# GpSimd rounds the gate weights, the compressed scores move into the GLA levels, and a Tanh goes ahead of the logarithms

## The chip, the cores and the metric

The kernel runs on one core of a Trainium2 chip. The metric is the device time of the whole program in microseconds, the median of several runs. Engines run their own instruction streams and meet at semaphores: TensorE (PE), VectorE (DVE), ScalarE (ACT), GpSimd (POOL), and SyncE (SP), which here issues the loads of weights.

## The reference, cut to what matters

The program has two blocks. The change touches only the first one, which runs two layers (`DEPTH = 2`) over 256 tokens of width 1024. One layer is:

```python
def hybrid_layer(x, ...):
    proj = rms_norm(x, norm_mix) @ w_in            # q, k, v, gates of all four mixers
    y_nsa = nsa_mixer(...)        # compressed + selected + window attention, 8 heads
    y_sb  = stick_breaking_mixer(sb_q, sb_k, sb_v)
    y_gla = gla_mixer(...)        # gated linear attention, 4 heads
    y_fox = forgetting_mixer(...)
    branch = einsum('bsnc,ncd->bsnd', stack([y_nsa, y_sb, y_gla, y_fox], axis=2), w_branch)
    gates  = sigmoid(gate_logits + b_gate)         # 4 x 1024 columns of proj
    x = x + sum(gates * branch) @ w_out
    return x + square(relu(rms_norm(x, norm_ff) @ w_ff1)) @ w_ff2

# nsa_mixer, compressed part: 15 compressed keys
s_cmp = einsum('bsghd,bcgd->bghsc', q, kc) * scale
p_cmp = masked_softmax(s_cmp, cmp_end[None, :] <= tok[:, None])
o_cmp = einsum('bghsc,bcgd->bsghd', p_cmp, vc)

# stick_breaking_mixer
sp = where(valid, softplus(z), 0)                  # needs a logarithm
later = cumsum(sp, reverse=True) - sp
a = where(valid, exp(log_sigmoid(z) - later), 0)
```

The second block (a modulated transformer with grouped and latent attention) is not touched by the change.

## The kernel before, in words

**Split products.** A product in float32 is made of three fast matmuls: each weight half tile (256 columns by 8 pieces of 128 rows, 128x2048 in SBUF) is split into a rounded high part and the rest. `Split.make_high` (L233 to L241) rounds on ScalarE into one of two buffers, `ring_high`; `Split.make_low` (L243 to L249) subtracts on VectorE, in place in the ring. Part i may be rounded when TensorE is done with part i-2, since there are two buffers. The parts are numbered: 26 for the projections, then 16 for the eight gate tiles (`GATE_CUT` is 26), then 4 for `w_out` (`OUT_CUT` is 42).

**The order in a layer.** It is written out by hand, engine by engine. TensorE makes the projections. Among those of the stick-breaking and forgetting mixers (names `sq0` to `fv1`) it puts nine *levels* of the gated linear attention (`level(n)`, L724 on). For each level VectorE runs `prepare(n)` (a difference, then, after an Abs and an Exp by ScalarE, two products), `make_low` of the next part, and `merge(n-1)`; ScalarE runs `level_exp`, takes a projection out of PSUM and runs `make_high`. Then come `ff` (two 8-column products per piece), the GLA output `go0`, `go1`, and the sum `fc` for the forgetting mixer.

**The steps.** 16 steps follow (`PAIRS`), m = 0 to 15. Step m has a pair of heads of one kind, in the order slc, win, fox, sb, four times over. In a step TensorE makes two gate projections (`filler`, g0 to g31, 24 matmuls of 256 columns each), the scores of this pair, the transposes (or, for sb, the sums, L842) of the pair before, and the output of the pair before. ScalarE takes each gate projection out of PSUM with a Tanh, makes the exponentials, and on odd fillers rounds a gate part for two steps later. VectorE makes maxima, normalisation and `make_low`. In an sb step ScalarE needs Abs and Exp, then two Ln, and the Ln lie in another function table than Exp and Tanh.

**The compressed scores.** TensorE makes them before the levels, into the two score banks (`cmp0`, `cmp1`). VectorE takes them (L1390) only after the GLA normalisation; s0, s1 of step 0 use the same two banks. TensorE transposes the weights `p_cmp` in step 1 (`turn_compressed`, L793), and ScalarE copies them from there. PSUM banks are used in a fixed rotation (`Banks`): a claim waits until the use two before is freed. g1 uses the bank of `fc`, g8 that of g7.

Of the kernel before, what the change touches and what calls it, by code (L numbers as in the profile page):

```python
# [14 lines left out]
P = 128  # L15
D, S, DEPTH = 1024, 256, 2
KD = D // P
# [189 lines left out]
class Split:  # L207
# [34 lines left out]

    def make_low(self, nc, dve, *which):  # L243
# [51 lines left out]
def first_layer(nc, l, T, dram, out, sem, chip):  # L295
# [91 lines left out]
    for i in range(4 * KD):  # L387
# [5 lines left out]
        if i in ada_steps:  # L393
# [21 lines left out]
               [f"rope{i}" for i in range(3)] + LV + ["p0", "p1"] + [f"pc{g}{i}" for g in range(2) for i in range(2)]  # L415
               + [f"p{j}" for j in soft_jobs[2:]])
# [122 lines left out]
    with nc.Block() as block:  # L539
# [27 lines left out]
        def _(pe):  # L567
# [199 lines left out]

            PT.taken(pe, "lv8_0", "lv8_1")
# [23 lines left out]

            def turn_compressed():  # L793

                for g in range(2):
                    pe.wait_ge(cmp_ready, g + 1)
                    for i in range(2):
                        ps = PT.claim(pe, f"pc{g}{i}")
                        for c in range(2):
                            for t in range(TT):  # L800
                                at = (c * TT + t) * P
                                last = turn(ps[0:N_CMP, at:at + P], p_cmp[:, g, 2 * i + c, t, :])
                        last.then_inc(PT.full, 1)
# [97 lines left out]
            for m in range(PAIRS + 1):  # L901
# [13 lines left out]
                if m == 1:  # L915
                    turn_compressed()
# [62 lines left out]
        def _(act):  # L979
# [115 lines left out]
            for i, (name, out, kw) in enumerate((  # L1095
# [8 lines left out]
                if 2 <= i + 1 <= len(LEVELS) - 2:  # L1104
                    level_exp(i + 1)
            PROJ.taken(act, "ff")
# [11 lines left out]
            for g in range(2):  # L1118
                act.wait_ge(cmp_in, g + 1)
                f(p_cmp[:, g], p_cmp[:, g], ACT.Exp).then_inc(cmp_exp, 1)  # L1120
# [3 lines left out]
            def filler(i):  # L1124
# [3 lines left out]
                if i % 2 == 1 and i < 4 * KD - 4:  # L1128
                    Y.make_high(nc, act, GATE_CUT + 2 + i // 2)
# [23 lines left out]
            def scores(m):  # L1153
                if jobs[2 * m][0] == "sb":
# [4 lines left out]
                    for e in range(2):  # L1159
                        f(sb_u[:, e], sb_u[:, e], ACT.Ln, bias=one).then_inc(sb_log, 1)  # L1160
                    return
                for e in range(2):
# [5 lines left out]
                      accum_out=total[:, e, 1:2]).then_inc(SC.free(f"s{j}"), 1)  # L1168

# [7 lines left out]
            for m in range(PAIRS + 1):  # L1177
# [11 lines left out]
                if m == 1:  # L1189
                    for g in range(2):  # L1190
                        for i in range(2):
                            ps = PT.arrived(act, f"pc{g}{i}")
                            copy(pcT[g][0:N_CMP, 2 * i:2 * i + 2, :], ps[0:N_CMP, :].rearrange("p (c s) -> p c s", c=2))\
                                .then_inc(PT.free(f"pc{g}{i}"), 1)
# [1340 lines left out]
```

## Time and profile before

| | us |
|---|---|
| median of 3 runs | 2514.04 |
| lowest and highest | 2513.93, 2516.71 |
| the profiled execution's own time | 2516.49 |
| its span, first to last instruction | 2514.7 |
| TensorE busy | 2289.3 (91%) |
| VectorE busy | 1122.4 (45%) |
| ScalarE busy | 1084.2 (43%) |
| GpSimd busy | 16.3 (1%) |
| mean granted TensorE clock | 0.96 of full |

The first layer lies at about 25 to 735 us of the span, the second at about 735 to 1450. Within them the levels lie at 133 to 209 and 845 to 921, the steps at 233 to 444 and 945 to 1159. A busy TensorE is not TensorE at its peak: the same matmuls take about twice as long at half the granted clock.

### The profile page before, as it was taken

The numbers are of one execution on the slowest core, as the hardware profiler recorded it, in microseconds if no ns is written. First come the engines' busy times: TensorE is split into PE (matmuls) and PEld (weight loads), VectorE is DVE, ScalarE is ACT, GpSimd is POOL, SyncE is SP. The second block draws the span as 40 slices with busy tenths as digits, with TensorE's granted clock in tenths as the row PEclk, the third lists the DMA queues.
The fourth block names the chain that finished last, engine by engine and source line by source line (L and its number), as shares of the span: only waits on it lengthen the run. The fifth ranks groups of instructions, "written<-read, shape, count | busy, mean of one in ns | idle before, by whom it ended". The sixth has DMA issues, their size and how long they took to land. (4 is left out here: it accounts for less than half of the span.)

```text
span 2514.7 us, 33045 instructions
## 1 busy us (share of the span) xinstructions
PE 2289.3 (91%) x13767; PEld 1845.2 (73%) x13767; DVE 1122.4 (45%) x1582; ACT 1084.2 (43%) x1720; POOL 16.3 (1%) x23
## 2 busy tenths in 40 slices
PE   5998999989969998999899798788999998997998
PEld 4898777879858996778798653445788886454987
DVE  3464333455424544342544312755334435265565
ACT  4444555156323445552464236742332241353553
POOL 0000000000000000000000000000000000100000
PEclk9998999999979998999899989998999999998999
DMA  7532566444446324656445242002222223212442
GB/s 201 200 135 101 197 224 203 175 180 177 167 109 217 131 81 176 216 201 218 167 168 187 80 182 72 2 1 84 101 101 82 86 78 88 71 64 84 167 174 78
DMA packets 197141, 341.19 MB, mean 136 GB/s; under 512 B 45955, under 2 KB 60734, under 8 KB 196862
## 3 DMA queue, kind: packets, MB, share of 16 engines
q1 hardware_dynamic: 194300, 334.68, 38.3%
q0 software_dynamic: 944, 3.47, 0.4%
q8 instruction: 112, 1.84, 0.3%
q10 hardware_dynamic: 1746, 0.89, 0.1%
q14 instruction: 39, 0.32, 0.0%
HBM read 335.88 MB, written 3.15 MB: 135 GB/s over the span
## 5 line engine op out<-in xcount | busy, mean ns | idle before, releaser
L261 PE MATMUL bank<-hT_high,ring_low 128*128 128x256 f32 (+1 forms) x2032 | 609.9, 300 | 0.0
L261 PEld LDWEIGHTS bank<-hT_high,ring_low 128*128 128x128 f32 x2032 | 394.0, 194 | 12.5 <-issue 0.5
L260 PE MATMUL bank<-hT_low,ring_high 128*128 128x256 f32 (+1 forms) x1008 | 300.1, 298 | 19.9 <-ACT work L983 11.7
L262 PE MATMUL bank<-hT_high,ring_high 128*128 128x256 f32 (+1 forms) x1008 | 291.6, 289 | 0.0
L248 DVE TENSOR_TENSOR ring_low<-ring,ring_high 128x2048 fp32r<-128x2048 f32 (+2 forms) x92 | 203.0, 2207 | 190.9 <-ACT ring_high L241 190.5
L260 PE MATMUL bank<-ring_low,hidden_high 128*128 128x512 f32 x640 | 254.3, 397 | 0.0
L241 ACT ACTIVATE ring_high<-ring 128x2048 fp32r<-128x2048 f32 (+2 forms) x92 | 169.2, 1841 | 154.4 <-DMA ring<-w_out 72.1
L260 PEld LDWEIGHTS bank<-hT_low,ring_high 128*128 128x128 f32 (+1 forms) x1008 | 197.4, 196 | 31.1 <-issue 19.6
L983 ACT ACTIVATE work<-bank 128x512 f32<-128x512 f32 (+8 forms) x264 | 120.4, 482 | 215.7 <-PE bank L262 172.4
L248 DVE TENSOR_TENSOR ring_low<-ring,half_high 128x2048 fp32r<-128x2048 f32 x64 | 146.3, 2292 | 136.6 <-ACT half_high L241 136.6
L262 PEld LDWEIGHTS bank<-hT_high,ring_high 128*128 128x128 f32 (+1 forms) x1008 | 196.6, 195 | 0.4
L241 ACT ACTIVATE half_high<-ring 128x2048 fp32r<-128x2048 f32 x64 | 121.7, 1908 | 154.1 <-PE bank L262 154.1
L260 PE MATMUL bank<-hT_low,half_high 128*128 128x512 f32 (+1 forms) x512 | 176.2, 344 | 11.6 <-DVE hT_low L2395 8.2
L262 PE MATMUL bank<-hT_high,half_high 128*128 128x512 f32 (+1 forms) x512 | 174.4, 341 | 0.0
L262 PE MATMUL bank<-half_high,hidden_high 128*128 128x512 f32 x384 | 151.5, 395 | 0.0
L261 PE MATMUL bank<-half_high,hidden_low 128*128 128x512 f32 x384 | 150.7, 392 | 0.0
L1831 PE MATMUL bank<-work,ring 128*128 128x512 f32 (+3 forms) x384 | 141.5, 524 | 6.8 <-DVE work L2241 3.7
L983 ACT ACTIVATE work<-bank,work 128x256 f32<-128x256 f32 (+1 forms) x200 | 88.1, 460 | 134.3 <-PE bank L262 95.5
L2065 ACT ACTIVATE work<-bank 128x512 f32<-128x512 f32 (+3 forms) x145 | 79.4, 584 | 143.3 <-PE bank L1831 140.7
L260 PEld LDWEIGHTS bank<-ring_low,hidden_high 128*128 128x128 f32 x640 | 120.2, 188 | 26.3
L569 PE MATMUL bank<-work 64*128 64x128 f32 (+8 forms) x1032 | 118.7, 334 | 21.3 <-DVE work L1390 14.9
L1831 PE MATMUL bank<-work 128*64 128x256 f32 (+5 forms) x550 | 111.7, 455 | 14.0 <-DVE work L2282 6.7
(214 smaller groups left out, 4153.1 us busy)
## 6 DMA issues: line engine op xcount, KB each, us to landing
ring<-w_ff SPq DMA_DIRECT2D x32, 2048.0 KB, 8.3
ring<-mlp_w SPq DMA_DIRECT2D x32, 2048.0 KB, 8.2
ring<-w_in SPq DMA_DIRECT2D x30, 2048.0 KB, 7.8
ring<-w_ada SPq DMA_DIRECT2D x24, 2048.0 KB, 7.9
ring<-w_branch SPq DMA_DIRECT2D x6, 2048.0 KB, 10.7
ring<-w_in SPq DMA_DIRECT2D x32, 256.0 KB, 4.2
ring<-w_out SPq DMA_DIRECT2D x4, 2048.0 KB, 7.7
ring<-gqa_w_qkv SPq DMA_DIRECT2D x3, 2048.0 KB, 15.6
```

Of the source, the lines that this page charges most:

```text
L241: nc.scalar.activation(self.high(i), self.part(i, False), ACT.Copy).then_inc(self.high_made, 1)
L248: nc.vector.tensor_tensor(self.part(i, True), self.part(i, False), self.high(i).bitcast(F32), ALU.subtract)\
L260: nc.tensor.matmul(out, a[0], b[1], start=start, stop=False)
L261: nc.tensor.matmul(out, a[1], b[0], start=False, stop=False)
L262: return nc.tensor.matmul(out, a[0], b[0], start=False, stop=stop)
L569: return nc.tensor.matmul(out, lhsT, rhs, start=start, stop=stop)
L983: return nc.scalar.activation(out, in_, func, **kw)
L1831: return nc.tensor.matmul(o, lhsT, rhs, start=start, stop=stop)
L2065: return f(o, src, ACT.Copy, **kw)
```

## The change

Three things are moved. (1) Of the 16 gate parts, ScalarE still rounds the first two; the other 14 are rounded by a copy on GpSimd, in a block of its own. (2) The work on the compressed scores goes into the GLA levels on VectorE and ScalarE; TensorE transposes `p_cmp` right behind `ff`, ahead of the GLA output, and ScalarE's four copies stand ahead of the `log_f` chain. The turn banks are rotated in the new order. (3) In an sb step ScalarE's two Ln (`logs(m)`) come at the end of the step, behind the Tanh of the odd gate filler and the copy of an output.

```diff
+    def round_high(self, nc, pool, i):
+        self.weights.arrived(pool, self.parts[i][0])
+        pool.wait_ge(self.high_made, i)
+        pool.wait_ge(*self.freed[i - len(self.buffers)])
+        nc.gpsimd.tensor_copy(self.high(i), self.part(i, False)).then_inc(self.high_made, 1)
...
+               [f"rope{i}" for i in range(3)] + LV + [f"pc{g}{i}" for g in range(2) for i in range(2)]
+               + [f"p{j}" for j in soft_jobs])
...
 # TensorE, behind ff (the function is moved as it is)
+            turn_compressed()
             PT.taken(pe, "lv8_0", "lv8_1")
             PROJ.taken(pe, "gv0", "gv1")
...
 # ScalarE, in the loop over the twelve projections
                 if 2 <= i + 1 <= len(LEVELS) - 2:
                     level_exp(i + 1)
+                if i in (4, 5):
+                    act.wait_ge(cmp_in, i - 3)
+                    f(p_cmp[:, i - 4], p_cmp[:, i - 4], ACT.Exp).then_inc(cmp_exp, 1)
+            for g in range(2):
+                for i in range(2):
+                    ps = PT.arrived(act, f"pc{g}{i}")
+                    copy(pcT[g][0:N_CMP, 2 * i:2 * i + 2, :], ...).then_inc(PT.free(f"pc{g}{i}"), 1)
             PROJ.taken(act, "ff")
             log1p_exp_neg_abs(log_f, fox_t).then_inc(fox_log, 1)
...
-                if i % 2 == 1 and i < 4 * KD - 4:
-                    Y.make_high(nc, act, GATE_CUT + 2 + i // 2)
...
-                    for e in range(2):
-                        f(sb_u[:, e], sb_u[:, e], ACT.Ln, bias=one).then_inc(sb_log, 1)
                     return
...
                 if m >= 1:
                     output(m - 1)
+                if m < PAIRS:
+                    logs(m)
+            act.wait_ge(Y.high_made, OUT_CUT)
             Y.make_high(nc, act, OUT_CUT, OUT_CUT + 1)
...
+        @block.gpsimd
+        def _(pool):
+            for i in range(GATE_CUT + 2, OUT_CUT):
+                Y.round_high(nc, pool, i)
...
 # VectorE: cmp_scores is L1390 to L1394 as it was, cmp_weights is L1396 to L1401
                 merge(n - 1)
+                if n in (3, 4):
+                    cmp_scores(n - 3)
+                if n in (6, 7):
+                    cmp_weights(n - 6)
```

VectorE before, in the levels: from one merge over the differences and products of a level to the next merge (`ring_low` is the low part of a weight tile, `masks` the level mask).

```order
L1337 COPY_PREDICATED work<-masks,bank 128x512 x2
L1323 TENSOR_TENSOR work<-work 128x512
L1326 TENSOR_TENSOR work<-work 128x512
L1327 TENSOR_TENSOR work<-work 128x512
L248 TENSOR_TENSOR ring_low_50<-ring,ring_high_53 128x8x256
L1337 COPY_PREDICATED work<-masks,bank 128x512 x2
```

VectorE now, at the same place (the line numbers are those of the changed kernel):

```order
L1353 COPY_PREDICATED work<-masks,bank 128x512 x2
L1378 TENSOR_TENSOR work<-work,consts 128x120
L1379 TENSOR_REDUCE work<-work 128x8
L1380 TENSOR_SCALAR work<-work 128x8
L1381 RECIPROCAL work<-work 128x8
L1382 TENSOR_TENSOR work<-work 128x8
L1383 TENSOR_TENSOR work<-work 128x120
L1339 TENSOR_TENSOR work<-work 128x512
L1342 TENSOR_TENSOR work<-work 128x512
L1343 TENSOR_TENSOR work<-work 128x512
L255 TENSOR_TENSOR ring_low_50<-ring,ring_high_53 128x8x256
L1353 COPY_PREDICATED work<-masks,bank 128x512 x2
```

Six small instructions stand between a merge and the next level's difference, in two of the levels; in two others it is the three of `cmp_scores`.

ScalarE before, in step 3 (an sb step), from the second score tile (Abs, Exp) over the Ln, the Tanh of g7, a rounding and two copies to the Tanh of g8:

```order
L983 ACTIVATE work<-bank 128x384
L983 ACTIVATE work<-work 128x384
L983 ACT_TABLE_LOAD
L983 ACTIVATE work<-work,consts 128x384 x2
L983 ACT_TABLE_LOAD
L983 ACTIVATE work<-bank,work 128x256
L241 ACTIVATE ring_high_54<-ring 128x2048
L983 ISA
L983 ACTIVATE mod<-bank 128x8
L983 ACTIVATE work<-bank 128x256
L983 ACTIVATE work<-bank,work 128x256
```

ScalarE now, in the same step:

```order
L991 ACTIVATE work<-bank 128x384
L991 ACTIVATE work<-work 128x384
L991 ACTIVATE work<-bank,work 128x256
L991 ISA
L991 ACTIVATE mod<-bank 128x8
L991 ACTIVATE work<-bank 128x256
L991 ACT_TABLE_LOAD
L991 ACTIVATE work<-work,consts 128x384 x2
L991 ACT_TABLE_LOAD
L991 ACTIVATE work<-bank,work 128x256
```

The Tanh of g7 and both copies have passed ahead of the Ln, and the rounding is gone.

TensorE before, in step 1: the transposes of `p_cmp` (15x128) between those of the GLA output and the output matmuls of step 0.

```order
L262 MATMUL bank<-hT_high,ring_high_54 128x256
L572 MATMUL bank<-consts,work 128x128 x4
L572 MATMUL bank<-consts,work 15x128 x16
L569 MATMUL bank<-work 64x256 x4
L569 MATMUL bank<-work 64x128 x2
```

TensorE now, behind the last product of `ff`:

```order
L269 MATMUL bank<-ring_high_54,hT_high 128x8
L579 MATMUL bank<-consts,work 15x128 x16
L576 MATMUL bank<-work 128x128 x12
L576 MATMUL bank<-consts,work 8x256
L576 MATMUL bank<-consts,work 8x128
L267 MATMUL bank<-hT_low,ring_high_53 128x256
```

The 16 transposes stand ahead of the twelve GLA output matmuls; nothing is left of them in step 1.

## Rows read from the trace of the kernel before

**Rows 1.** Stretches: length, busy us of PE, PEld, DVE, ACT, POOL, PEclk, DMA share, GB/s.
```profile
244.50:248.50 4.00, 3.99 (x21) 3.35 (x22) 2.98 (x13) 1.94 (x8) 0.00 (x0) 0.50 0.00 0
265.30:273.80 8.50, 8.48 (x48) 6.27 (x48) 1.16 (x1) 1.52 (x3) 0.00 (x0) 0.60 0.44 170
320.00:370.00 50.00, 48.06 (x409) 39.22 (x408) 20.00 (x41) 28.73 (x62) 0.00 (x0) 1.00 0.64 226
955.60:962.60 7.00, 6.99 (x40) 6.22 (x41) 4.57 (x20) 2.64 (x11) 0.00 (x0) 0.54 0.00 0
1106.00:1113.80 7.80, 7.59 (x38) 7.43 (x39) 2.29 (x1) 3.17 (x7) 0.00 (x0) 0.60 0.58 217
```

**Rows 2.** Waits of PE, 290 to 445: who for whom, us in total, times, longest.
```profile
PE bank L260 <- ACT work L983: 5.8, 3, 1.9
```

**Rows 3.** Timeline, PE, ff to step 1: start, us, instruction, idle before it.
```profile
228.26 4.50 PE L569 MATMUL bank<-work 128*128 128x128 f32 x24
244.51 1.65 PE L569 MATMUL bank<-work 64*128 64x128 f32 x8 [7.94 <-DVE work L1390]
246.46 0.56 PE L260 MATMUL bank<-hT_low,ring_high 128*128 128x256 f32 x1
261.67 1.47 PE L572 MATMUL bank<-consts,work 128*128 128x128 f32 x12
265.32 1.52 PE L572 MATMUL bank<-consts,work 128*15 128x128 f32 x8 [2.18 <-ACT work L983]
269.29 0.58 PE L260 MATMUL bank<-hT_low,ring_high 128*128 128x256 f32 x1
```

**Rows 4.** Waits of PE in the levels, 170 to 228.
```profile
PE bank L569 <- DVE work L1337: 2.2, 4, 0.9
```

**Rows 5.** Timeline, DVE, differences of two levels and a low part.
```profile
186.23 0.69 DVE L1323 TENSOR_TENSOR work<-work 128x512 f32<-128x512 f32 x1
190.57 2.29 DVE L248 TENSOR_TENSOR ring_low<-ring,ring_high 128x2048 fp32r<-128x2048 f32 x1 [1.00 <-ACT ring_high L241]
194.21 0.69 DVE L1323 TENSOR_TENSOR work<-work 128x512 f32<-128x512 f32 x1
```

**Rows 6.** Timeline, DVE, the compressed scores of group 0.
```profile
241.34 0.27 DVE L1390 TENSOR_TENSOR work<-bank,consts 128x120 f32<-128x120 f32 x1
242.61 0.28 DVE L1396 TENSOR_TENSOR work<-work,consts 128x120 f32<-128x120 f32 x1 [0.37 <-ACT work L983]
243.89 0.28 DVE L1401 TENSOR_TENSOR work<-work 128x120 f32<-128x120 f32 x1
```

**Rows 7.** Timeline, ACT, one copy in the levels.
```profile
172.19 0.60 ACT L983 ACTIVATE work<-bank 128x512 f32<-128x512 f32 x1 [1.41 <-PE bank L262]
```

**Rows 8.** Timeline, ACT, from the last rounding before the steps.
```profile
228.50 1.91 ACT L241 ACTIVATE ring_high<-ring 128x2048 fp32r<-128x2048 f32 x1 [6.39 <-PE bank L262]
232.29 0.26 ACT L983 ACTIVATE work<-bank 128x128 f32<-128x128 f32 x1
240.06 0.21 ACT L983 ACTIVATE work<-work 128x4 f32<-128x4 f32 x1
```

**Rows 9.** Timeline, ACT, table loads and Ln of steps 3 and 15.
```profile
292.60 1.28 ACT L983 ACT_TABLE_LOAD   x1
293.90 1.12 ACT L983 ACTIVATE work<-work,consts 128x384 f32<-128x384 f32 x2
...
438.07 1.12 ACT L983 ACTIVATE work<-work,consts 128x384 f32<-128x384 f32 x2
```

**Rows 10.** Timeline, PE, g8 and the last sums.
```profile
296.95 0.55 PE L260 MATMUL bank<-hT_low,ring_high 128*128 128x256 f32 x1 [1.94 <-ACT work L983]
...
439.33 2.02 PE L842 MATMUL bank<-work,consts 128*128 128x256 f32 x12 [0.15 <-DVE work L1410]
```

**Rows 11.** Copies on POOL by form: shapes, count, busy us, mean ns, idle before.
```profile
L2442 POOL COPY work<-work 32x2048 f32<-32x2048 f32 x4 | 7.4, 1886 | 47.6 <-DVE work L2273 47.6
L2426 POOL COPY work<-work 64x512 f32<-64x512 f32 x8 | 4.9, 609 | 1511.9 <-DVE work L2273 1511.5
```

More of the change, by code:

```diff
@@ L765, in _, with turn_compressed @@
             last.then_inc(PROJ.full, 1)
+            def turn_compressed():
+                for g in range(2):
+                    pe.wait_ge(cmp_ready, g + 1)
+                    for i in range(2):
+                        ps = PT.claim(pe, f"pc{g}{i}")
+                        for c in range(2):
+                            for t in range(TT):
+                                at = (c * TT + t) * P
+                                last = turn(ps[0:N_CMP, at:at + P], p_cmp[:, g, 2 * i + c, t, :])
+                        last.then_inc(PT.full, 1)
+            turn_compressed()
             PT.taken(pe, "lv8_0", "lv8_1")
@@ L1105, in _ @@
                     level_exp(i + 1)
+                if i in (4, 5):
+                    act.wait_ge(cmp_in, i - 3)
+                    f(p_cmp[:, i - 4], p_cmp[:, i - 4], ACT.Exp).then_inc(cmp_exp, 1)
+            for g in range(2):
+                for i in range(2):
+                    ps = PT.arrived(act, f"pc{g}{i}")
+                    copy(pcT[g][0:N_CMP, 2 * i:2 * i + 2, :], ps[0:N_CMP, :].rearrange("p (c s) -> p c s", c=2))\
+                        .then_inc(PT.free(f"pc{g}{i}"), 1)
             PROJ.taken(act, "ff")
@@ L1168, in scores, with logs @@
                       accum_out=total[:, e, 1:2]).then_inc(SC.free(f"s{j}"), 1)
+            def logs(m):
+                if jobs[2 * m][0] == "sb":
+                    for e in range(2):
+                        f(sb_u[:, e], sb_u[:, e], ACT.Ln, bias=one).then_inc(sb_log, 1)
             def output(m):
@@ L1345, in silu_gate, with cmp_scores, cmp_weights @@
                 link(vec.scalar_tensor_tensor(gle[:, t, :], gle[:, t, :], 1.0, glg[:, t, :], ALU.add, ALU.mult))
+            bias = K("cmp_bias").rearrange("p (t n) -> p t n", t=TT).unsqueeze(1).to_broadcast([P, 4, TT, N_CMP])
+            seen = K("cmp_seen").rearrange("p (t n) -> p t n", t=TT).unsqueeze(1).to_broadcast([P, 4, TT, N_CMP])
+            def cmp_scores(g):
+                ps = SC.arrived(dve, f"cmp{g}")
+                pc, st = p_cmp[:, g], stat_cmp[:, g]
+                vec.tensor_tensor(pc, ps[:, 0:4 * TT * N_CMP].rearrange("p (c t n) -> p c t n", c=4, t=TT), bias, ALU.add)\
+                    .then_inc(SC.free(f"cmp{g}"), 1)
+                SC.taken(dve, f"cmp{g}")
+                link(vec.tensor_reduce(st, pc, axis=AX.X, op=ALU.max))
+                vec.tensor_tensor(pc, pc, st.unsqueeze(3).to_broadcast([P, 4, TT, N_CMP]), ALU.subtract).then_inc(cmp_in, 1)
+            def cmp_weights(g):
+                pc, st = p_cmp[:, g], stat_cmp[:, g]
+                dve.wait_ge(cmp_exp, g + 1)
+                link(vec.tensor_tensor(pc, pc, seen, ALU.mult))
+                link(vec.tensor_reduce(st, pc, axis=AX.X, op=ALU.add))
+                link(vec.tensor_scalar_max(st, st, 1e-30))
+                link(vec.reciprocal(st, st))
+                link(vec.tensor_tensor(st, st, nsa_gate[:, 0, 4 * g:4 * g + 4, :], ALU.mult))
+                vec.tensor_tensor(pc, pc, st.unsqueeze(3).to_broadcast([P, 4, TT, N_CMP]), ALU.mult).then_inc(cmp_ready, 1)
             prepare(0)
```

41 lines of the change are left out of this document (removed).

## The prediction
> **What bounds the kernel now.** I read first the granted clock and busy time of stretches, then TensorE's waits, then the timelines of TensorE, ScalarE and VectorE about each wait. In the steps TensorE is busy 48.06 of 50 us at full clock [rows 1]: it is the bound there, and ScalarE, at 28.73 us, is not. Work taken off ScalarE gains only where TensorE waits for it. There are four such places in each layer, and a fifth where the change adds a wait:
> - Before step 0, s0 waits 7.94 us for VectorE to empty the bank of the compressed scores [rows 3].
> - In step 1 the transposes of p_cmp wait 2.18 us for ScalarE's copies [rows 3].
> - Behind three sb steps, g8 and its like wait 1.94 us each, 5.8 in all [rows 2, 10]: g8 needs g7's bank, and g7's Tanh stands behind two Ln and two table loads [rows 9].
> - At the end the last sums wait for the last Ln, by only 0.15 us [rows 10].
> - In the later levels TensorE waits 2.2 us in four times for VectorE's merge [rows 4]. VectorE and ScalarE form a loop there, whose round takes 194.21 - 186.23 = 7.98 us [rows 5]. Difference, Exp, copy, rounding, low part and merge all follow each other in it, so what is put into this loop is paid in full.
>
> After each of these waits the clock stood at its lower level (1.2 GHz) for a while: 0.50 in 244.5:248.5, 0.60 over the 8.5 us from 265.3, 0.54 and 0.60 in two stretches of the second layer [rows 1]. A stretch of length L at mean clock c loses about L(1 - c): 2.0, 3.4, 3.2 and 3.1 us.
>
> **Levels: +4.1 us a layer.** cmp_scores is 242.61 - 0.37 - 241.34 = 0.90 us of VectorE, with the next start 0.93; cmp_weights is 243.89 + 0.28 - 242.61 = 1.56 [rows 6]; the Exp costs about 0.3 (VectorE waited 0.37 for it). The two cmp_scores lengthen the loop by 1.86, but ScalarE then waits for TensorE's fifth projection anyhow, with 1.41 to spare [rows 7], so about 0.4 is left. The rest, two Exp and two cmp_weights, has no cover: 2 x (0.30 + 1.56) = 3.7. Late next is TensorE's level, whose bank waits for the merge, and everything behind it. Bounds: 0 (if a slack hides it) and 5.6 (the sum). I take 4.1; two layers 8.2.
>
> **From ff to g1: -3.1 a layer.** Call the end of ff T, 228.4. ScalarE's last rounding waits for it and ends at T + 2.0 [rows 8]. Now four copies of 15x512 stand behind it; with 0.60 us for one [rows 7], and the third and fourth transposes waiting for the first and second copy, they end near T + 4.4. TensorE's GLA output starts at about T + 3.7 instead of T, but that is not what g1 waits for. g1 needs the bank of fc, and ScalarE copies fc only at the end of its chain. From the end of the rounding (230.4) to the last Exp at 240.06 + 0.21 [rows 8] that chain took 9.9 us; it now ends at T + 14.3, is followed by the fc copy (about 0.4) and no longer by two waits for VectorE. g1 starts near T + 14.9, against 246.46 - 228.4 = T + 18.1 [rows 3]. Scores s0, free of the 7.94 us wait, fit in between. TensorE still idles for about 1.5 us before g1.
>
> **Step 1: -7.15 a layer.** TensorE's 12 transposes from 261.67 are four of the GLA output, to about 262.15, and eight of p_cmp. Then came 2.18 of waiting, and 8.5 us at clock 0.60 [rows 1, 3] for eight more transposes, the output and g4. From 262.15 to 273.8 that is 11.65. At full clock the last stretch is 8.5 - 3.4 = 5.1, and without its eight transposes (about 0.6 to 1.0) near 4.5. 11.65 - 4.5 = 7.15; two layers 14.3. The transposes have been counted in the part above.
>
> **Logarithms: -5.8 a layer inside, +2.9 at the end.** In step 3 TensorE's output ends at 296.95 - 1.94 = 295.01 [rows 10]. g7's Tanh now comes before that, so g8 starts at once. ScalarE copies the output (0.4), loads the table (1.28), and from the first Ln to the sums TensorE needs 439.33 - 438.07 = 1.26 [rows 9, 10]: they can start at 298.0, and g8 ends near 298.1, if it takes 3.1 us (fc and g0 took 244.51 - 7.94 - 232.76 = 3.8 together [rows 3], g0 about 3.1 of it). The cover just suffices. In step 15 no filler follows. Output ends at 439.18, and by the same 0.4 + 1.3 + 1.26 and small gaps the sums start at 442.2 instead of 439.33: +2.9, passed on to the branch products, which need the last outputs. Both layers: -11.6 and +5.8.
>
> **Rounding on GpSimd: 0.** The 14 roundings (1.9 us each on ScalarE [rows 8]) are hidden before and must be after. No row shows this cast on GpSimd. The nearest are copies of float32: 32x2048 in 1.886 us, 64x512 in 0.609 [rows 11]. The time goes by elements per partition in these two, which gives 1.9 us; scaled by partitions it would be 4 x 1.886 = 7.5. What is free: part i may start when part i-2 is done, at the end of an odd filler, and is needed at the start of the even filler two steps later. That is about a step, (439.33 - 246.46) / 15 = 12.9 us in the mean [rows 3, 10], less 2.3 for VectorE's low part [rows 5]: 10.6 us. Both bounds fit. I take 0. VectorE waits in its order for the rounding, and behind it stand the next step's maxima, due about a step less a filler later (12.9 - 3.1 = 9.8 us), with some slack on TensorE after them. Loads don't move against this: the queue on SP waits for TensorE's own ends.
>
> A price from a page alone: the Trainium skill (GPSIMD Engine Reference, 3.1 Elementwise) gives 4497 ns for a two-input add of 2048 float32 on GpSimd; taking that for the cast, as an estimate, the sum would stay the same, since it is under 10.6.
>
> **Clock: -3.5 in all.** Besides step 1's, the losses behind waits that go were 2.0, 3.2 and 3.1 us. Shorter waits now stand elsewhere (about 2 us twice in each layer's levels, 1.5 before g1), and one of 1.94 was enough to bring the clock down in the second layer (the last of these losses) [rows 1]. Bounds -8 and +4; I take less than half the gain.
>
> **Sum.** 8.2 - 6.2 - 14.3 - 11.6 + 5.8 + 0 - 3.5 = -21.6. The profiled execution took 2516.5 in a span of 2514.7; with it 2494.9. The median lies 2.5 below that execution: **2492**.
>
> **Rivals.**
> 1. The Ln come too late. The cover of g8 has 0.1 us to spare; if TensorE waits for the sums as long as it waited for g8, the 11.6 are lost and the end stays: 2504. For it: three waits in a row on ScalarE (output, table, Ln). Against: each has its row, and the excess would have to be 1.9 us six times.
> 2. The levels have slack. If the loop is not what TensorE waits for, the 8.2 don't come: 2484. For it: TensorE's waits there are only 0.45 us or so. Against: a wait for the merge in four of the levels, so the slack is negative already.
> 3. Slower than before: the cast on GpSimd outlasts its cover. Place: each of the 28 gate parts. Price: 28 x (d - 10.6) us for a cast of d us; it makes the kernel slower from d = 11.4 on, and at 14 us the time is 2492 + 95 = 2587. For it: the operation turns float32 into the rounded type, which no row shows. Against: 6 times the row.
>
> The Trainium skill (SBUF — State Buffer, SBUF: two separate sides) says that GpSimd and VectorE share a port pair, and whoever starts first holds it for the whole instruction. A cast could then start up to one low part (2.3 us) late, and rival 3 would decide from 9.1 us instead; I know of no row here that shows the two at once, and give rival 3 a little more for it.
>
> **Chances.** Forecast as summed, 2484 to 2500 with its clock term: 0.66. Rival 1: 0.16. Rival 2: 0.12. Rival 3: 0.04. No change at all, by something not seen: 0.02. What a measurement of this kernel can tell is about 0.2%, 5 us; so faster is all below 2509: 0.66 + 0.16 + 0.12 less a little for a rival 1 with bad clock, 0.92; the same 0.04, slower 0.04. The range takes in rival 1 and most of rival 2: 2482 to 2506.
>
> **What would show it.** On GpSimd 28 casts of 128x2048, each below 10 us; behind them no wait of TensorE for ring_low. TensorE's wait for VectorE before s0 gone, and one of 1 to 3 us before g1 in its place. The merge waits in the levels near 1.2, 0.8, 2.3 and 2.0 instead of four short ones. Nothing between the GLA transposes and the output in step 1. In steps 4, 8 and 12 no wait before the even filler, and none above 0.3 us before L842's counterpart; in step 15 one of about 3 us. If the sb waits merely move, or the time from 240 to 270 does not shrink by 7 us or more in each layer, I am wrong.

## The result, and the profile after

| us | before | after |
|---|---|---|
| median | 2515.38 (2513.93 to 2517.28, 4 runs) | 2501.18 (2499.27 to 2501.85, 4 runs) |
| the profiled execution, its span | 2516.49, 2514.7 | 2499.27, 2497.4 |

The median of before has one run more than the table ahead of the prediction. The ratio is 0.994, with a 95% interval of 0.9924 to 0.9956: the change makes the kernel faster by 14.2 us. The forecast was 2492, within 2482 to 2506. The direction and the mechanism came, two thirds of the size (14.2 of 22 us) did.

The page of after, busy time by engine. ScalarE has 47 us less than before, GpSimd 54 more:

```profile
PE 2291.5 (92%) x13767; PEld 1841.8 (74%) x13767; DVE 1123.5 (45%) x1582; ACT 1037.3 (42%) x1692; POOL 70.4 (3%) x51
```

Below are the stretches of after that answer to [rows 1] (columns as there), in this order: about the longest wait in the levels; the steps; the last sums of both layers with what surrounds them:

```profile
196.00:206.00 10.00, 9.58 (x70) 9.20 (x71) 7.31 (x13) 4.43 (x6) 0.00 (x0) 0.83 0.52 192
320.00:370.00 50.00, 50.00 (x424) 40.67 (x423) 20.13 (x47) 23.34 (x66) 9.62 (x5) 1.00 0.64 230
429.30:434.50 5.20, 4.50 (x20) 3.64 (x20) 0.44 (x1) 2.13 (x3) 0.00 (x0) 0.68 1.03 423
1130.80:1140.50 9.70, 5.36 (x22) 4.01 (x21) 1.06 (x2) 5.43 (x8) 0.00 (x0) 0.58 1.02 421
```

In the steps TensorE is busy for all of the 50 us, where it was 48.06: nothing is left to win there by moving other engines' work. At the end of the steps the clock is low now (0.68 and 0.58), where it was at full in the kernel before.

TensorE's timeline of after, about the places of [rows 3] and [rows 10] (start, us, instruction, idle before it):

```profile
196.03 2.09 PE L576 MATMUL bank<-work 64*128 64x128 f32 x16 [2.09 <-DVE work L1353]
232.76 1.87 PE L579 MATMUL bank<-consts,work 128*15 128x128 f32 x8
235.53 1.87 PE L579 MATMUL bank<-consts,work 128*15 128x128 f32 x8 [0.90 <-ACT work L991]
248.28 0.36 PE L267 MATMUL bank<-hT_low,ring_high 128*128 128x256 f32 x1 [1.22 <-ACT work L991]
...
263.02 1.45 PE L576 MATMUL bank<-work 15*64 15x256 f32 x12
264.40 0.39 PE L267 MATMUL bank<-hT_low,ring_high 128*128 128x256 f32 x1
...
429.29 3.65 PE L852 MATMUL bank<-work,consts 128*128 128x256 f32 x12 [3.00 <-DVE work L1432]
...
435.14 1.10 PE L576 MATMUL bank<-work,ring 128*128 128x256 f32 x4 [0.67 <-ACT work L991]
```

The 7.94 us before s0 and the 2.18 us in step 1 are gone; 1.22 us stand before g1. The last sums (L852, the sums of `sb` that were L842) wait 3.00 us instead of 0.15, and then run for 3.65 us instead of 2.02.

The waits of TensorE in after, in the levels (170 to 232, against [rows 4]) and then in the steps (285 to 440, against [rows 2]):

```profile
PE bank L576 <- DVE work L1353: 4.0, 4, 2.1
...
PE bank L852 <- DVE work L1432: 3.0, 1, 3.0
PE bank L576 <- ACT work L991: 1.3, 2, 0.7
```

The last row is not new: the kernel before has 1.5 us in two waits there, about the last output.

The cause in the levels is in VectorE's timeline of after: the first of the six small instructions between a merge and the next level's difference, and that difference, which starts 1.49 us later for them:

```profile
196.57 0.28 DVE L1378 TENSOR_TENSOR work<-work,consts 128x120 f32<-128x120 f32 x1
...
198.06 0.69 DVE L1339 TENSOR_TENSOR work<-work 128x512 f32<-128x512 f32 x1
```

ScalarE's timeline of after, the output's copy and the Ln of step 3 and of step 15 (against [rows 9]). Only a table load lies between them now.

```profile
288.71 0.38 ACT L991 ACTIVATE work<-bank 128x256 f32<-128x256 f32 x1 [0.54 <-PE bank L576]
...
290.41 1.12 ACT L991 ACTIVATE work<-work,consts 128x384 f32<-128x384 f32 x2
...
426.33 0.38 ACT L991 ACTIVATE work<-bank 128x256 f32<-128x256 f32 x1 [0.54 <-PE bank L576]
...
428.02 1.12 ACT L991 ACTIVATE work<-work,consts 128x384 f32<-128x384 f32 x2
```

In step 3 TensorE fills this time with g8; in step 15 there is nothing to fill it with.

GpSimd's first two casts in after. The forecast had no row of such a cast (its nearest were [rows 11]):

```profile
251.53 1.89 POOL L248 CAST ring_high<-ring 128x2048 fp32r<-128x2048 f32 x1 [251.07 <-PE bank L269]
262.81 2.03 POOL L248 CAST ring_high<-ring 128x2048 fp32r<-128x2048 f32 x1 [9.40 <-PE bank L269]
```

**One table for all kernels.** I cut the profiled execution of every kernel at the same instructions of TensorE: the first matmul of level 5; the end of the last product of ff; the start of g1; the end of g4; the end of the output before the last sums; the start of the branch products. What lies outside of these (the rest) is the same code of TensorE in all of them. First and second layer, us, worked out from the timelines:

```
                    levels       ff to g1     g1 to g4     steps          end         sum     rest
before              50.71 49.60  18.06 18.07  27.38 28.77  165.34 168.28  4.58 4.59   535.4   1979.3
after               54.68 54.63  15.38 15.37  19.21 20.74  158.79 158.79  8.86 9.68   516.1   1981.3
e2 rounding only    50.93 51.18  18.07 18.06  22.76 22.55  165.56 165.53  4.59 4.59   523.8   1979.6
e3 scores only      54.67 53.89  15.38 15.38  19.21 19.20  164.04 168.29  4.58 4.58   519.2   1982.3
e4 logs only        49.74 49.60  18.07 18.07  28.68 24.21  160.89 160.88  9.67 9.00   528.8   1990.7
e1 no rounding      54.64 54.78  15.38 15.38  20.73 19.21  160.88 160.87  8.81 8.71   519.4   1984.4
e11 no scores       50.09 49.92  18.09 18.09  23.56 23.71  158.81 158.82  9.68 9.68   520.5   1985.7
e5 last logs back   53.98 55.10  15.38 15.38  20.72 19.21  158.79 158.79  4.58 4.59   506.5   1984.8
e6 scores idle      49.85 50.94  15.38 15.39  19.22 20.75  158.78 158.79  8.76 9.67   507.5   1984.3
e7 three repairs    51.76 53.86  12.27 12.27  20.73 19.22  158.79 158.79  4.59 4.58   496.9   1982.7
e12 and part 27     54.37 54.02  10.70 10.69  19.20 19.21  158.79 158.79  4.58 4.59   494.9   1983.0
```

A stretch whose waits are the same comes out within some hundredths, unless a half-clock period falls into it; the steps of after do so to 0.01 us. From before to after, 19.25 us are gained in the table's stretches and 2.0 are lost outside of them.

The table has one execution of each kernel. The kernel before was run 17 times beside e1 to e4: from 2509.76 to 2520.62 us, with a mean granted clock between 0.961 and 0.956. So a few us of the rest, and of a stretch with a half-clock period in it, can belong to the execution and not to the kernel. A half-clock period is here a time in which the granted clock is 0.50.

### The profile page after: what moved, and what is told of

It reads as the page before. It is cut to its first block and busy times, and to the rows that moved or that the text cites. A ratio compares the mean times of both kernels' runs of the same rounds, so it can differ in the third digit from the quotient of the medians.

```text
span 2497.4 us, 33053 instructions
## 1 busy us (share of the span) xinstructions
PE 2291.5 (92%) x13767; PEld 1841.8 (74%) x13767; DVE 1123.5 (45%) x1582; ACT 1037.3 (42%) x1692; POOL 70.4 (3%) x51
## 3 DMA queue, kind: packets, MB, share of 16 engines
q8 instruction: 112, 1.84, 0.3%
## 5 line engine op out<-in xcount | busy, mean ns | idle before, releaser
L268 PEld LDWEIGHTS bank<-hT_high,ring_low 128*128 128x128 f32 x2032 | 390.2, 192 | 12.5 <-issue 0.5
L267 PEld LDWEIGHTS bank<-hT_low,ring_high 128*128 128x128 f32 (+1 forms) x1008 | 193.3, 192 | 23.3 <-issue 12.1
L267 PE MATMUL bank<-hT_low,half_high 128*128 128x512 f32 (+1 forms) x512 | 176.3, 344 | 11.7 <-DVE hT_low L2417 8.2
L241 ACT ACTIVATE ring_high<-ring 128x2048 fp32r<-128x2048 f32 (+2 forms) x64 | 115.9, 1814 | 156.6 <-DMA ring<-w_out 74.1
L1853 PEld LDWEIGHTS bank<-work,ring 128*128 128x128 f32 (+2 forms) x384 | 70.1, 185 | 73.7 <-issue 63.6
```

The source lines that it names most:

```text
L241: nc.scalar.activation(self.high(i), self.part(i, False), ACT.Copy).then_inc(self.high_made, 1)
L267: nc.tensor.matmul(out, a[0], b[1], start=start, stop=False)
L268: nc.tensor.matmul(out, a[1], b[0], start=False, stop=False)
L1853: return nc.tensor.matmul(o, lhsT, rhs, start=start, stop=stop)
```

## The experiments

Each was timed in five rounds against the kernel before on the same chip. The median of before was 2517.51 (17 runs) for e1 to e4, 2517.77 (11) for e5 to e8, 2515.96 (13) for the last four; so I go by the ratios, and for the mechanism by the table. Differences between medians of two groups can be off by some 2 us, by which those of before differ.

### The parts alone: e1 to e4, e11

**e1, the changed kernel with the roundings back on ScalarE.** The GpSimd block goes, and:

```diff
                 f(gates[:, i, :], ps[:, 0:S], ACT.Tanh, ...)
+                if i % 2 == 1 and i < 4 * KD - 4:
+                    Y.make_high(nc, act, GATE_CUT + 2 + i // 2)
```

> The changed kernel with the 14 gate roundings of a layer back on ScalarE, at their old place behind the Tanh; the rest as changed. Theory: in an sb step the rounding now stands between the Tanh of the odd filler and the output copy, table load and Ln, so the Ln end about 1 us later than their cover (g8's 3.1 us) and TensorE waits about 1 us for the sums in steps 4, 8, 12 of both layers: 6 us slower than the changed kernel, about 2507. Rival (GpSimd is only an idle hand, its move is worth nothing): 2501, no wait before the sums.

Measured: 2505.49 (2503.25 to 2506.83, 6 runs), ratio 0.9954 (0.9938 to 0.9969), some 4 us above the changed kernel; the theory had 6. The reason is in step 3; ScalarE's and then TensorE's timeline of e1:

```profile
289.69 1.90 ACT L241 ACTIVATE ring_high<-ring 128x2048 fp32r<-128x2048 f32 x1
...
291.55 0.38 ACT L991 ACTIVATE work<-bank 128x256 f32<-128x256 f32 x1
```
```profile
294.50 2.02 PE L852 MATMUL bank<-work,consts 128*128 128x256 f32 x12 [0.68 <-DVE work L1428]
```

The rounding stands ahead of the output's copy, and the Ln stand behind that copy. They now end later than g8 covers, and the sums wait 0.68 us three times a layer (steps 160.88 against 158.79 in the table). The rival, which had no wait there, is out.

**e2, only the roundings moved to GpSimd**; scores and Ln stand as before.

> The kernel before with only the 14 roundings moved to GpSimd. Theory: the 1.94 us waits behind the sb steps stay, since the Tanh still stands behind the Ln; in step 1 ScalarE's copies of the compressed transposes come about 1.8 us earlier, so the 2.18 us wait nearly goes: 3 to 5 us faster than before, about 2511. Rival (off the path altogether): 2515. Rival (the port that VectorE and GpSimd share stalls VectorE on the path): slower than 2517.

Measured: 2505.85 (2504.98 to 2509.03, 6 runs), ratio 0.996 (0.9945 to 0.9976). The gain is larger than either side of the expectation had it. The table puts most of it into g1 to g4, 4.62 and 6.22 us, and the timelines of e2 say why, TensorE's first, then ScalarE's first two copies of p_cmp:

```profile
263.86 1.03 PE L579 MATMUL bank<-consts,work 128*15 128x128 f32 x8 [0.47 <-ACT work L990]
```
```profile
263.14 1.05 ACT L990 ACTIVATE work<-bank 15x512 f32<-15x512 f32 x2
```

In the kernel before, the first two copies of p_cmp came behind a rounding of 1.9 us on ScalarE:

```profile
262.24 1.90 ACT L241 ACTIVATE ring_high<-ring 128x2048 fp32r<-128x2048 f32 x1
264.04 0.68 ACT L983 ACTIVATE work<-bank,work 128x512 f32<-128x512 f32 x1
264.61 1.05 ACT L983 ACTIVATE work<-bank 15x512 f32<-15x512 f32 x2
```

Without it TensorE waits 0.47 us instead of 2.18 [rows 3], and no half clock follows. So the rounding was paid for in step 1, and I had costed its removal at nothing.

**e3, only the scores moved**, into the levels as in the change.

> The kernel before with only the compressed scores moved (levels on VectorE and ScalarE, transposes behind ff). Theory, from the two traces: levels +4.0 and +5.0, ff to g1 -2.7 twice, g1 to the end of g4 about -8.1 twice: -12.6, about 2503. Rival (most of the gain is that of the logarithms): 2509 or more.

Measured: 2503.81 (2501.61 to 2506.97, 6 runs), ratio 0.9952 (0.9936 to 0.9968), as expected. The table has the levels' loss (3.96 and 4.29), the gain before g1 (2.68 and 2.69) and the gain in step 1 (8.17 and 9.57).

**e4, only the Ln moved**, roundings on ScalarE and scores as before:

```diff
                         link(f(sb_u[:, e], sb_u[:, e], ACT.Exp, scale=-1.0))
-                    for e in range(2):
-                        f(sb_u[:, e], sb_u[:, e], ACT.Ln, bias=one).then_inc(sb_log, 1)
                     return
...
                     output(m - 1)
+                if m < PAIRS:
+                    logs(m)
```

> The kernel before with only the two Ln of the sb steps moved to the end of the step; ScalarE still rounds. Theory: the 1.94 us waits before g8, g16, g24 go, but the rounding delays the Ln past their cover, so about 1 us of wait appears before the sums each time, and the last step costs 4 to 5 us in each layer: -12 + 6 + 9 with some clock given back, about 2515, the same as before. Rival (the Ln are covered without the rounding's move): 2509.

Measured: 2520.47 (2518.56 to 2524.85, 12 runs), ratio 1.0019 (1.0008 to 1.003): no gain, rather a small loss. The waits came as the theory had them: those of 1.94 us are gone, and the sums wait 5.0 us in four times in each layer, as in e1. In the layers it gains 6.6 us by the table: the steps are shorter by 4.45 and 7.40, the end is longer by 5.09 and 4.41, and a half-clock period is missing from step 1 of the second layer. It loses 11.4 us in the rest, where no instruction differs. The two long stretches of the rest, of before and then of e4:

```profile
443.76:889.89 446.13, 405.46 (x2678) 366.54 (x2678) 205.16 (x199) 179.37 (x206) 0.00 (x0) 0.95 0.47 160
1159.20:2514.70 1355.50, 1246.63 (x5940) 928.93 (x5940) 622.93 (x842) 545.44 (x817) 16.07 (x19) 0.96 0.29 103
```
```profile
446.15:895.76 449.61, 408.96 (x2677) 370.46 (x2678) 205.20 (x199) 179.35 (x206) 0.00 (x0) 0.94 0.45 154
1157.52:2519.50 1361.98, 1258.48 (x5940) 934.33 (x5940) 623.23 (x842) 545.74 (x817) 16.12 (x19) 0.96 0.28 101
```

VectorE and ScalarE do the same work in the same time; TensorE is busy 3.5 and 11.9 us longer for the same matmuls. Its clock is lower there: summed over the trace's clock record, the rest has 143 us at half clock in the kernel before, 152 in the changed one and 177 in e4. Two of e4's periods begin about the late sums of step 15 and reach 2.9 and 5.0 us into the rest (in the changed kernel one does, by 5.5 us). For the others nothing in the program differs, and why they are longer stays open. The 12 runs say that not all of it is one execution's luck: by the medians e4 is 3.0 us slower, although its stretches gain 6.6.

**e11, rounding and Ln moved, the scores at their old place.**

> The changed kernel with the compressed scores back at their old place: the rounding on GpSimd and the Ln behind the Tanh alone. Theory (the rounding on GpSimd already takes most of step 1's wait and half clock away, so the moved scores add little to it): the steps save 6.5 us a layer, step 1 4.5, the end costs 4.3 to 5.1: about 13 us under the kernel before, 2503 to 2506, and the changed kernel is only 2 to 4 us below that. Rival (the parts add up as they did alone, rounding -11.7 and logarithms +3): 9 us under, 2509.

Measured: 2507.0 (2501.3 to 2511.41, 8 runs), ratio 0.9959 (0.9945 to 0.9974). That is 9 us under the kernel before by the medians, as the rival has it, and 10 by the ratio, whose interval (6.5 to 13.8 us) takes in the theory's 10 to 13 too; the times don't tell the two apart. The table is on the theory's side: g1 to g4 gains 3.82 and 5.06 in it, and 19.25 - (535.4 - 520.5) = 4.3 us are what the moved scores add to it inside the stretches. Rounding and scores take away one and the same wait in step 1: alone they give 10.8 and 17.7 us there, together 16.2. The moved scores by themselves take all of it, the rounding about two thirds.

### The two losses undone: e5, e6, e7, e12

**e5, the Ln of step 15 back behind their Exp**, the others left where the change put them:

```diff
                         link(f(sb_u[:, e], sb_u[:, e], ACT.Exp, scale=-1.0))
+                    if m == PAIRS - 1:
+                        logs(m)
                     return
...
-                if m < PAIRS:
+                if m < PAIRS - 1:
                     logs(m)
```

> The changed kernel with one thing undone: in step 15 of each layer the two Ln stand again right behind the Exp of the scores, ahead of the Tanh; in steps 3, 7 and 11 they stay behind the Tanh and the output's copy. Theory (the late Ln of the last step cost 3.00 us of waiting and the half clock after it: from the last output to the branch products 8.86 and 9.68 us against 4.58 before): the wait before the last sums falls to about 0.15 us, the stretch to 4.6, and the program takes 9 us less than the changed kernel, about 2492. Rival (the wait only passes to something else that comes as late, the branch products or the table loads): within 3 us of the changed kernel.

Measured: 2491.96 (2487.81 to 2493.11, 4 runs), ratio 0.9892 (0.9878 to 0.9906). TensorE's timeline of e5:

```profile
428.57 2.02 PE L852 MATMUL bank<-work,consts 128*128 128x256 f32 x12 [0.15 <-DVE work L1434]
431.46 0.87 PE L576 MATMUL bank<-work 128*64 128x256 f32 x8 [0.87 <-ACT work L991]
```

The end is 4.58 us again in both layers, 9.4 us less by the table, where the theory had 9. The program's time says it less sharply: 9.2 us less by the medians, 12 by the ratios, and 6.1 between the two profiled executions, since the rest of e5 is 3.5 us longer.

**e6, the compressed scores in VectorE's idle time** behind the last low part of the projections, ScalarE's Exp behind the copy of fv0:

```diff
-                if n in (3, 4):
-                    cmp_scores(n - 3)
-                if n in (6, 7):
-                    cmp_weights(n - 6)
...
             Y.make_low(nc, dve, 25)
+            for g in range(2):
+                cmp_scores(g)
+            for g in range(2):
+                cmp_weights(g)
```

> The changed kernel with the work on the compressed scores out of the loop of the levels: VectorE does both scores and both weights behind the low part 25, where it idles until the GLA output comes, and ScalarE does the two Exp behind the copy of fv0. The transposes and ScalarE's copies stay where the change put them. Theory (the levels lengthened by 3.97 and 5.03 us because that work stands in the loop of VectorE and ScalarE that TensorE waits for): the waits for the merge are again 0.86, 0.45, 0.45, 0.45, the levels are as long as in the kernel before, and the program takes 8 to 9 us less than the changed kernel, about 2492. Rival (the 16 transposes behind ff and their 0.90 us wait are what was paid, not the loop): under 3 us less.

Measured: 2492.7 (2491.32 to 2502.48, 6 runs), ratio 0.9908 (0.9892 to 0.9923): 8.5 us under the changed kernel by the medians, 8 by the ratios. TensorE's waits in the levels of e6, 170 to 228:

```profile
PE bank L576 <- DVE work L1354: 2.2, 4, 0.9
```

That is the row of the kernel before [rows 4], with the gains in ff to g1 and in step 1 kept. The transposes behind ff and their 0.90 us wait are as in the changed kernel, so the rival is out: what was paid stood in the loop.

**e7, both, with the 16 transposes between the products of fv and ff on TensorE** and ScalarE's four copies ahead of its last rounding.

> Both of the last two, and TensorE's 16 transposes of p_cmp between the products of fv and of ff, with ScalarE's four copies ahead of its last rounding. Theory: the sum of the two gains, 18 us, and another 2 us a layer from the log_f chain, which has four copies less ahead of it and is what g1 waits for: 2479, between 2475 and 2485. Rival (what is taken away in one place comes back as a wait at the next, at g1 above all): no better than the better of the other two, 2490 to 2492.

Measured: 2480.08 (2479.74 to 2481.38, 5 runs), ratio 0.985 (0.9838 to 0.9863), 21 us under the changed kernel and 37.7 under the one before. ff to g1 falls by a further 3.11 us. The transposes, 1.03 us for eight, now lie in the stretch before. It takes 51.76 us with them in the first layer and 53.86 in the second, where it also has 5.5 us at half clock.

**e12, e7 with the rounding of part 27 on GpSimd too.** It was the last rounding ahead of the log_f chain that g1 waits for.

> The version with all three repairs, and the rounding of the second gate part (the last one that ScalarE did ahead of the log_f chain, 1.91 us behind ff) on GpSimd too. Theory (g1 waits 1.76 and 2.19 us for a ScalarE chain that begins behind this rounding): the chain ends 1.9 us earlier, the wait before g1 is gone or under 0.4 us, and the program takes 3.5 to 5 us less, 2475.5 (2474 to 2477.5). Rival (the chain waits next for VectorE, whose low parts a cast holds up, or for the sums of log_f): under 2 us less, 2478 or more.

Measured: 2479.82 (2477.46 to 2481.48, 4 runs), ratio 0.9856 (0.9838 to 0.9875): the same as e7, as the rival had it, but not for its reason. ff to g1 did fall by 1.57 us, though g1 still waits 1.12 us for ScalarE, where the theory had at most 0.4. The stretch before it became longer by 2.61 in the first layer. Windows over the products of ff, of e12 and of e7; then GpSimd and VectorE in e12:

```profile
225.00:233.00 8.00, 8.00 (x46) 8.00 (x46) 0.00 (x0) 0.50 (x2) 0.00 (x0) 0.60 0.00 0
```
```profile
224.30:229.30 5.00, 5.00 (x43) 5.00 (x42) 0.00 (x0) 0.01 (x1) 0.00 (x0) 0.90 0.00 0
```
```profile
233.32 1.89 POOL L248 CAST ring_high<-ring 128x2048 fp32r<-128x2048 f32 x1 [232.87 <-PE bank L269]
233.35 4.01 DVE L255 TENSOR_TENSOR ring_low<-ring,ring_high 128x2048 fp32r<-128x2048 f32 x1
```

The clock is low in e12 for most of the products of ff, and in e7 only from near their end: the instructions are the same, where the half-clock period falls is not. In the second layer, where it falls alike (54.02 and 53.86), e12 is ahead by 1.4 us at the start of g1. So the chain's gain is there. In the first layer the clock takes more than all of it up to g1 (1.0 us behind), and gives 1.5 back in step 1. In sum the stretches are 2.0 us shorter than in e7, which the times do not resolve. The low part, 2.29 us alone [rows 5], takes 4.01 us beside the cast, and TensorE did not wait for it.

### How long may a cast be: e8, e10, e9

Each cast is repeated within its turn:

```diff
+        for _ in range(2):
+            self.again += 1
+            nc.gpsimd.tensor_copy(self.high(i), self.part(i, False)).then_inc(self.pool_self, 1)
+            pool.wait_ge(self.pool_self, self.again)
         nc.gpsimd.tensor_copy(self.high(i), self.part(i, False)).then_inc(self.high_made, 1)
```

(2 for three casts, 4 and 5 for five and six.)

> The changed kernel with each of the 28 roundings on GpSimd done three times over, one behind the other, into the same buffer: a rounding of about 5.8 us in place of 1.9. Theory (10.6 us are free for a rounding in each step): GpSimd is busy for 162 us in casts instead of 54, and the time stays within 0.2% of the changed kernel, 2501. Rival A (the cover is shorter than 5.8 us because VectorE waits in its order for the rounding): 28 x 1 us or more, over 2525. Rival B (small operations of VectorE are held for as long as a cast runs, as the one of 128x2 that took 1.84 us in place of 0.16; three casts catch three times as many of them): slower by 3 to 15 us.

> The same with five: about 9.5 us each. Theory (10.6 us are free): within 0.2% of the changed kernel, 2501 to 2505. Rival (the port pair that GpSimd and VectorE share takes a low part of 2.3 us out of the cover, so it ends at 8.3): 28 x 1.2 = 34 us more, 2535.

> The changed kernel with each rounding on GpSimd done six times over: about 6 x 1.91 = 11.5 us each. Theory (10.6 us are free, what is over it is paid 28 times): 28 x 0.9 = 25 us more than the changed kernel, 2515 to 2535, and TensorE waits for ring_low in the steps. Rival A (VectorE's slack in its order stretches the cover, since low parts can come later than the sum took them): under 5 us more. Rival B (the roundings are in a chain with VectorE's work, and a longer one also delays maxima and normalisations): over 40 us more.

| casts | us of GpSimd in one rounding, mean | median us | ratio to before |
|---|---|---|---|
| 1 | 1.9 | 2501.18 (2499.27 to 2501.85, 4 runs) | 0.994 (0.9924 to 0.9956) |
| 3 | 5.7 | 2502.09 (2501.64 to 2506.61, 5 runs) | 0.9946 (0.9933 to 0.9959) |
| 5 | 10.1 | 2553.55 (2549.03 to 2556.23, 4 runs) | 1.0148 (1.0128 to 1.0169) |
| 6 | 12.6 | 2600.17 (2594.51 to 2607.22, 5 runs) | 1.0334 (1.0313 to 1.0355) |

Three casts cost nothing that these runs resolve, as expected. Five cost 52 us where the theory had none and the rival 34; six cost 99 where the theory had 25 and rival B over 40. So the edge of the prediction's rival 3 is real, and nearer than 11.4 us: it lies between 5.7 and 10.1, where the 9.1 of the prediction's port argument lies too. The timelines of GpSimd, VectorE and TensorE in e10 (five casts), from four of the casts of one rounding to the transposes:

```profile
300.18 9.97 POOL L251 CAST ring_high<-ring 128x2048 fp32r<-128x2048 f32 x4
304.30 1.88 DVE L1451 TENSOR_SCALAR work<-work 128x128 f32<-128x128 f32 x1
306.55 1.66 DVE L1450 TENSOR_TENSOR work<-work 128x2 f32<-128x2 f32 x1
308.24 1.99 DVE L1451 TENSOR_SCALAR work<-work 128x128 f32<-128x128 f32 x1
310.63 0.87 PE L584 MATMUL bank<-consts,work 128*128 128x128 f32 x3 [3.53 <-DVE work L1452]
```

TensorE waits here for a normalisation, not for ring_low. The normalisation stands behind the low part in VectorE's order, and it is itself held up by the casts, as the casts are by it (four in 9.97 us). Such waits come to 12.5 and 13.2 us in the two layers, and none of TensorE's waits in e10 is for ring_low. Only with six casts does that wait come as well (10.1 and 10.9 us, beside 14.0 and 12.1 for the normalisation).

That is both mechanisms of the expectations in one: a cover that ends earlier, and an order in which a late low part takes the softmax with it. How much each has was not separated. What can be separated is the clock: from g1 to the branch products TensorE idles 34.6 us longer in e10 than in the changed kernel, and 56.9 us longer in e9. The stretches of the table are 52 and 94 us longer; the remaining 17 and 37 us are the same matmuls at a lower clock. The 34.6 us are near the rival's 34, but it had them as waits for ring_low, so that is luck.

## Why the prediction came out as it did

**By its terms**, both layers, the profiled executions (the forecast's -21.6 was against the same execution of before):

| term | forecast | measured |
|---|---|---|
| levels | +8.2 | +9.0 |
| ff to g1 | -6.2 | -5.4 |
| step 1 (g1 to g4) | -14.3 | -16.2 |
| Ln, inside the steps | -11.6 | -16.0 |
| Ln, at the end | +5.8 | +9.4 |
| rounding | 0 | in the two above |
| clock | -3.5 | in the others |
| the rest | 0 | +2.0 |
| sum | -21.6 | -17.3 |

- **The bound was read rightly.** All five places named are where the time changed, and in the steps TensorE is left without a wait.
- **Levels: right.** The loop argument gave 4.1 a layer; 3.97 and 5.03 came. Of these the loop itself has 3.3 in both layers: levels 5 to 8 start 8.17, 9.63 and 9.45 us apart, against three times 7.98 before. The two rounds with a cmp_weights in them are longer by 1.65 and 1.47 us, where I had 1.86 each with the Exp. The other 0.66 and 1.71 us are lost behind level 8, where the changed kernel has more time at half clock. That the sum met 4.1 in the first layer is in part luck. Rival 2 (slack) is out: e6 takes just this work out of the loop and gets it back. The waits are 0.85, 0.64, 2.09 and 0.39, in sum 4.0, where I had given 6.3: behind the third the clock is lower (0.83 in 196:206), and TensorE spends in slower products what I had put into the fourth wait. The second layer of e8 (three casts) shows it: there the clock stays at full behind the third wait, level 8 starts 9.45 us behind level 7 all the same, and the fourth wait is 1.92 us:

```profile
911.30 1.68 PE L581 MATMUL bank<-work 64*128 64x128 f32 x16 [1.92 <-DVE work L1358]
```

- **ff to g1: right**, 2.68 and 2.70 for 3.1. g1 waits for the chain on ScalarE; e7 and e12 shorten that chain, and the stretch follows by 3.11 and 1.57. The copies in the chain end 0.7 us later than I had them, behind transposes that take 1.87 us for eight at half clock, where they take 1.03 in e7.
- **Step 1: right in size, its cause told by half.** I put the 2.18 us wait down to the place of the copies. e3 shows that moving them is enough. e2 shows that the wait was due to the rounding ahead of the copies as well: without it 0.47 us are left, with the scores where they were.
- **The Ln inside: the mechanism was right; the cover of 0.1 us just suffices**, so rival 1 is out. But it suffices only with the roundings gone: e1 and e4 have 0.68 us of wait three times a layer. The step "rounding on GpSimd: 0" was thus wrong as an account of what the rounding is worth. On top of the other two parts it is worth 4 us (e1), alone 11.7 (e2). The sum was not hurt, because the working of the other two terms had silently assumed the rounding gone. The further 4.4 us here are the half clock behind the old waits, above all that behind the third one of the second layer (the last stretch of [rows 1]), which I had in the clock term.
- **The end: the term that was mis-sized.** I forecast +2.9 a layer. The wait came as forecast, 3.00 against 0.15. What I left out is the lower clock behind it. With the clock at 0.68 and 0.58 in the two stretches shown (1.2 GHz for much of them) the sums take 3.65 and 3.78 us instead of 2.02, and in the second layer the output takes 1.55 instead of 0.87. The end costs 4.3 and 5.1 us, not 2.9, and e5 takes both back.
- **The clock: counted on one side only.** I took 3.5 us of net gain on top of the half clock in step 1's term. Behind the old waits more went than the terms had without it: 1.9 us in step 1 and 4.4 in the steps. Against that stand 3.6 us more at the end, 0.8 in the levels, 0.8 before g1, and 2.0 in the rest. The mean granted clock of the whole program is 0.96 before and after, so there was hardly a net gain. That each of these small differences is the clock's is shown for the end and for the levels; for the rest it is argued from its longer time at half clock (152 against 143 us).
- **The reference point.** I took the median to lie 2.5 us below the profiled execution. With more runs it lies 1.1 below it for before, and for after 1.9 above it. That makes the 3 us between -17.2 by the times of the executions (2516.49 and 2499.27) and -14.2 by medians.
- **GpSimd's cast: its length was right** (1.9 us, by elements per partition, as in [rows 11]). The page price of the Trainium skill (GPSIMD Engine Reference, 3.1 Elementwise) of 4497 ns for a two-input add is 2.4 times what this cast takes. The cover of 10.6 us was too long: I measured it to the low part and its filler, and in e10 the first thing TensorE waits for is the normalisation behind them. With a cast of 1.9 us this decided nothing.
- **Rival 3's port.** Of VectorE's small operations some are held while a cast runs, some not: in e10 the multiplication of 128x128 takes 1225 ns in the mean of 22 instead of 287, the RECIPROCAL of 128x2 161 instead of 164. That agrees with the Trainium skill (SBUF — State Buffer, SBUF: two separate sides): only operations of VectorE that use the shared port pair contend, and the first holder keeps it for its whole instruction. In the changed kernel it costs nothing that can be seen, in e12 1.7 us of one low part.

## What to carry to other kernels

Where the same instruction is late behind two others on an engine that works in order, moving either one away can give much or all of the gain (10.8 and 17.7 us here, 16.2 together), so price each part of a change both alone and on top of the rest. A step that is moved back behind other work is free only where the consumer has a filler to run; treat the last round of a loop on its own (9 us here for two lines), and look for idle time on the engine before putting small work into its critical loop (8.5 us). Count the half clock behind every new wait of some 3 us as you count it behind the waits that go.

## What the runs showed of the hardware

- One rounding of 128x2048 float32 takes about the same on GpSimd (1.89 to 2.04 us) as on ScalarE (1.91). It is no slower engine for this operation.
- While a cast runs, short operations of VectorE of some kinds are held, by up to 1.7 us. VectorE's groups between 250 and 440, in after and with five casts (mean ns before the second bar). With three they are 430 and 476 ns:

```profile
L1446 DVE TENSOR_SCALAR work<-work 128x128 f32<-128x128 f32 x24 | 6.9, 287 | 0.9
L1445 DVE TENSOR_TENSOR work<-work 128x2 f32<-128x2 f32 x16 | 4.3, 266 | 0.6
```
```profile
L1451 DVE TENSOR_SCALAR work<-work 128x128 f32<-128x128 f32 x22 | 27.0, 1225 | 0.8
L1450 DVE TENSOR_TENSOR work<-work 128x2 f32<-128x2 f32 x16 | 13.5, 842 | 0.5
```

  One of 128x2 took 1.84 us in the changed kernel, where it takes 0.16 in the kernel before. Low parts in the steps stay at 2.29 us throughout; it is the cast that is held there. In e10 the one that starts at 300.18, 0.09 us behind a low part, takes 3.96 us instead of 1.9.
- Waits that come again and again also cost clock. With five and six casts each rounding costs 52 / 28 = 1.9 and 99 / 28 = 3.5 us, and the mean clock of the whole program is 0.951 and 0.943, against 0.96 in the changed kernel.
- Moving work in one place shifted TensorE's half-clock periods in others where no instruction had changed, by up to 11 us in all (e4, a part of which follows its late sums). Effects of that size need the table by stretches before a cause is named.
